# Recurrent chunks of a 64-step linear recurrence: state product and state update moved from level 2 to level 4, GpSimd's operands moved between its mask products

## What is computed

```python
def rwkv7_step(state, inp):
    r_t, w_t, k_t, v_t, kk_t, a_t = inp
    sa = jnp.einsum('bhvk,bhk->bhv', state, -kk_t)
    state = (state * w_t[:, :, None, :] + sa[..., None] * (kk_t * a_t)[:, :, None, :]
             + v_t[..., None] * k_t[:, :, None, :])
    y = jnp.einsum('bhvk,bhk->bhv', state, r_t)
    return state, y
```

## Time and profile before

| | us |
|---|---|
| median of 3 runs | 2630.66 (2630.11 to 2630.99) |
| the profiled execution | 2630.19 |
| its span in the profile | 2628.2 |
| TensorE, matmul busy | 2567.8 (98%) |
| TensorE, weight loads busy | 2086.1 (79%) |
| VectorE busy | 1561.6 (59%) |
| ScalarE busy | 1108.6 (42%) |
| GpSimd busy | 425.6 (16%) |
| recurrent chunks, from the first to the last (2256 to 2509 us) | 253: weight loads busy 207.27 |

### The profile page before, as it was taken

How to read it: one execution, slowest core, us unless ns; L and a number is a source line. 1 busy time by engine, 2 the same in 40 slices (tenths; PEclk the granted TensorE clock), 3 DMA queues, 4 the chain that set the end, 5 groups by cost and what they waited for, 6 DMA issues and landing times.

```text
span 2628.2 us, 46698 instructions
## 1 busy us (share of the span) xinstructions
PE 2567.8 (98%) x19224; PEld 2086.1 (79%) x19224; DVE 1561.6 (59%) x2521; ACT 1108.6 (42%) x2067; POOL 425.6 (16%) x381
## 2 busy tenths in 40 slices
PE   8999999999999999999999999999999999999998
PEld 6887777778778998899888777766776677788876
DVE  8765443436686665676546676355567646656754
ACT  3242233323355543556335554324445545344521
POOL 4421221100000000000000000111112100456644
PEclk9999999999999999999999999999999999999999
DMA  6753443134423454534534222631011253100032
GB/s 227 212 119 107 97 131 101 65 115 165 160 102 116 144 192 141 189 132 150 170 127 173 76 96 90 270 129 49 29 49 49 85 189 105 42 19 19 19 129 96
DMA packets 80754, 307.24 MB, mean 117 GB/s; under 512 B 7200, under 2 KB 8864, under 8 KB 62624
## 3 DMA queue, kind: packets, MB, share of 16 engines
q1 hardware_dynamic: 55984, 238.72, 25.9%
q0 software_dynamic: 12800, 33.56, 5.6%
q10 hardware_dynamic: 11760, 31.99, 3.2%
HBM read 268.32 MB, written 69.47 MB: 129 GB/s over the span
## 4 chain that ended last, share of the span: by engine, by line
PE 83%; DVE 9%; ACT 4%; issue 3%; DMA 1%; POOL 1%; DVEq 0%; ACTq 0%; SPq 0%; POOLq 0%
PE ps L425 46%; PE ps L3270 4%; PE ps L1258 4%; PE ps L1257 4%; PE ps L1259 4%; PE ps L2145 2%; PE ps L2191 2%; PE ps L2171 2%; PE ps L2072 2%; PE ps L609 2%; PE ps L635 1%; PE ps L2074 1%; PE ps L2073 1%; PE ps L624 1%; DVE parts L404 1%
## 5 line engine op out<-in xcount | busy, mean ns | idle before, releaser
L425 PE MATMUL ps<-parts,parts 128*128 128x512 f32 (+2 forms) x6456 | 1467.5, 387 | 15.9 <-DVE parts L804 8.8
L425 PEld LDWEIGHTS ps<-parts,parts 128*128 128x128 f32 x6456 | 1171.6, 188 | 299.7 <-issue 34.3
L404 DVE TENSOR_TENSOR parts<-ring,parts 128x1024 fp32r<-128x1024 f32 x180 | 220.8, 1238 | 174.7 <-ACT parts L381 166.3
L381 ACT CAST parts<-ring 128x1024 fp32r<-128x1024 f32 x183 | 188.7, 1044 | 116.9 <-DMA ring<-in_weights 62.1
L1257 PE MATMUL ps<-parts,parts 128*128 128x256 f32 x840 | 236.2, 281 | 1.3 <-ACT phase_data L1406 1.3
L1258 PE MATMUL ps<-parts,parts 128*128 128x256 f32 x840 | 236.1, 281 | 0.0
L1259 PE MATMUL ps<-parts,parts 128*128 128x256 f32 x840 | 236.0, 281 | 0.0
L404 POOL TENSOR_TENSOR parts<-ring,parts 128x1024 fp32r<-128x1024 f32 x62 | 153.2, 2472 | 423.1 <-DVE parts L381 423.0
L2552 POOL TENSOR_TENSOR phase_data<-phase_data,stream 128x512 f32<-128x512 f32 x12 | 17.2, 1436 | 1186.2 <-PE ps L2082 1186.2
L867 DVE TENSOR_TENSOR_SCAN stream<-stream 128x513 f32<-128x513 f32 (+3 forms) x96 | 95.2, 992 | 173.2 <-ACT stream L737 173.0
L1257 PEld LDWEIGHTS ps<-parts,parts 128*128 128x128 f32 x840 | 158.7, 189 | 2.4 <-ACT phase_data L1406 1.5
(11 more groups left out here) (391 smaller groups left out, 3761.6 us busy)
## 6 DMA issues: line engine op xcount, KB each, us to landing
ring<-in_weights SPq DMA_DIRECT2D x128, 1024.0 KB, 4.9
up_sums<-in_weights POOLq DMA_DIRECT2D x24, 1024.0 KB, 8.9
ring<-in_weights SPq DMA_DIRECT2D x32, 512.0 KB, 4.3
ring<-up_sums SPq DMA_DIRECT2D x30, 512.0 KB, 5.9
phase_data<-up_sums SPq DMA_DIRECT2D x60, 256.0 KB, 5.6
up_sums<-up_sums POOLq DMA_DIRECT2D x8, 1024.0 KB, 5.4
phase_data<-in_weights SPq DMA_DIRECT2D x30, 256.0 KB, 5.5
raw_keep<-phase_scratch SPq DMA_DIRECT2D x21, 256.0 KB, 2.4
```

Of the source, the lines that this page charges most:

```text
L381: cast(self.hi(p), self.whole(p)).then_inc(self.k.hi_ready, 1)
L404: g.tensor_tensor(self.lo(p), self.whole(p), self.hi(p).bitcast(F32), ALU.subtract).then_inc(self.k.lo_ready, 1)
L425: last = pe.matmul(out, a, b, start=i == 0 and a is ah and b is bh, stop=i == len(pairs) - 1 and a is al)
```

## The change

`state_product(c - 1)` on TensorE and `next_state(c - 1)` on VectorE go from level 2 to level 4. `mean` goes from behind level 3 to behind level 4, with its wait as it was. On GpSimd the operands of the next chunk are made after the masks of levels 0 to 2 and before those of 3 to 5, and `bonus_in` and `lower` stand behind the masks. The wait for `x_mm` stays ahead of the first mask. No product is added or left out.

```diff
@@ -3378,11 +3378,12 @@
                     inv_x(c, l)
                     if l == 2 and c >= 1:
                         y_part(c - 1)
-                        state_product(c - 1)
                     if l == 3 and c + 1 < C:
                         raw(c + 1)
+                    if l == 4 and c >= 1:
+                        state_product(c - 1)
                     inv_w(c, l)
-                    if l == 3 and 8 <= c < 12:
+                    if l == 4 and 8 <= c < 12:
                         mean(c - 8)
                     if l == 3 and 9 <= c < 13:
                         bonus(c - 9)
@@ -3619,7 +3620,7 @@
-                    if l == 2 and c >= 1:
+                    if l == 4 and c >= 1:
                         next_state(c - 1)
@@ -3684,15 +3685,16 @@
         for c in range(C):
+            if c >= 2:
+                g.wait_ge(x_mm[1], LEVELS * (c - 1))
+            chunk_levels(k, g, chunk, c, range(0 if c else 1, 3))
+            if c + 1 < C:
+                operands(c + 1)
+            chunk_levels(k, g, chunk, c, range(3, LEVELS))
             if 8 <= c < 12:
                 bonus_in(c - 8)
             if c >= 12:
                 pieces.lower(g, c - 11)
-            if c >= 2:
-                g.wait_ge(x_mm[1], LEVELS * (c - 1))
-            chunk_levels(k, g, chunk, c, range(0 if c else 1, LEVELS))
-            if c + 1 < C:
-                operands(c + 1)
```

## The result

| | before | after |
|---|---|---|
| median of the runs, us | 2630.66 (2629.71 to 2631.09, 5 runs) | 2641.10 (2639.62 to 2643.78, 5 runs) |
| the profiled execution, us | 2630.19 | 2643.78 |
| its span, us | 2628.2 | 2641.9 |

The change makes the kernel slower: the ratio is 1.0041, with a 95% interval of 1.0027 to 1.0056, or +10.4 us. The forecast was 2635.4 (+4.7), in a range of 2631.5 to 2642.5. The time is in the range, and slower was the side with the larger chance, by 0.49 to 0.48.

The account below looks back on a forecast made before the run. The chunks were taken as a loop over TensorE, VectorE and ScalarE. Terms 0.4 + 5.77 - 0.56 - 1.0 + 0.1 = +4.7 us on 2630.19, plus 0.47 to the median, gave 2635.4 us, range 2631.5 to 2642.5.

Parts of the forecast that it names:

- The filler and the loop: Chunks 1 to 7 and 14: state product between x_4 and w_4, less 0.46 us saved in level 2; +0.05 us each.
- Mean's wait: Chunks 8 to 11, level 4: TensorE stands before mean until VectorE's update of the same chunk; together +5.77 us.
- the sum of chunk 9: Chunk 9, level 4 to the next chunk's state_part: 8.66 us instead of 7.22, +1.44; chunks 10 and 11 taken alike.
- The rival: Chunks 1 to 8 and 14: update's multiply waits for GpSimd's second mask, +0.66 us each, +5.9 together, 2641.3; chance 0.22.
- the missed turn: VectorE's update multiply, if 0.10 us later than thought, is let in only after GpSimd's second mask; +0.66 us per chunk.
- Chunks 12 and 13: No mean; VectorE comes late to the next chunk's start; about +0.1 us together, half a microsecond either way.
- Chunk 14: Counted with chunks 1 to 7 as a chunk without mean, +0.05 us.
- Chunks 0 and 15: Chunk 0: first raw's wait for GpSimd's operands goes, -0.56 us. Chunk 15: x_4's wait for the update's multiply shrinks, -1.0.
- the 1.48: Chunk 15: x_4's wait in us for the update's multiply before the change; it should be gone.
- the forecast's own case: Whole kernel: the summed terms hold, 2635.4 us with a spread of about 1.5 us; chance 0.68.

Follow-up runs that it names:

- the filler kernel: Changed kernel plus unread 128 x 512 products right ahead of mean, one in chunk 8, two in each of 9 to 11: 2639.84 us, ratio 1.0036.
- the kernel of the three repairs: Changed kernel with mean in PSUM bank 1, GpSimd's masks of chunks 10 to 13 behind the update, and x_keep's reload later: 2631.16 us, ratio 1.0002.
- The masks kernel: The filler kernel with GpSimd's masks of chunks 10 to 13 waiting for the update of chunks 9 to 12: 2637.58 us, ratio 1.0028.

## Why the prediction was right or wrong

**The filler and the loop** (+0.05 in each of the eight chunks without mean): right. x_4 to w_4 came out at 1.40, and chunks 1 to 7 grew by 0.06. Costing the product at 0.62 plus 0.07 for the change of tile, less what the copy hides, was the right reading.

**Mean's wait** (+5.77 in chunks 8 to 11): right in mechanism, and in size where nothing was on top of it, in chunk 8 (+1.45 forecast, +1.50 measured). Two kernels, one with mean in another bank and one with the old order there, are each only 2.5 to 2.8 us over before, and mean without the wait gives 16.04 and 17.73 in chunks 8 and 9, before's periods. What the forecast left out is that the wait makes TensorE idle long enough to be answered by the clock, and that VectorE's update, on which the wait hangs, has to share the SBUF with GpSimd.

**The step that failed** is the sum of chunk 9, "then 2.57 + 1.91 + 1.28", and "Chunks 10 and 11 as 9" behind it. Its 2.57 is the multiply at 0.42 and was 3.08; its 1.91 holds at full clock only. It forecast +1.44; without half clock it is +1.95 (19.73 against 17.78, in the filler kernel and, with no filler, in chunk 9 of the two kernels with `lower` at the end and with the reload later). The rival's mechanism, the missed turn, is this 0.5. I put the rival's question in chunks 1 to 8 and 14, where the multiply was in time: the next mask's record starts 0.037 us after it in chunk 2 and only 0.005 us after it in chunk 8. It was decided in chunks 9 to 12, which the rival didn't count. There the masks start at w_3 + 4.00, but inv_w of level 4 comes later: between w_3 and w_4 stands bonus, and w_3 to w_4 is 3.36 us (2408.18 - 2404.82) instead of 2.53. The multiply asks at w_3 + 5.41 and meets the third mask, not the first. The rival had the rule right for two tensor_tensor and looked at one place only. The masks held back until the update brought mean to w_4 + 2.54 from 3.08, and with mean in bank 1 holding back the masks is worth 0.94 in chunk 10 (18.67 against 17.73) and 0.56 in chunk 11 (18.67 against 18.11), for the multiply and finish's last step together.

**Left out: the clock.** Two stretches at 0.51 cost 1.6 us each in the profiled execution, 3.2 together, and one in the kernel with GpSimd's old loop. That they follow from the idle time before mean is shown by the filler, which fills it with useless work and shortens chunks 9 and 10, and by the kernels without the wait: at least one stretch in chunks 9 or 10 in each of the four kernels with the wait of 2.06 us, none in chunks 8 to 12 of the five without it. Each of these is one profiled execution. How often an execution has one or two of them is open; so is how much of the median they make, and the filler kernel's median (1.2 us below the kernel beside it) speaks for less than 3.2.

**Chunks 12 and 13** (+0.1, half a microsecond either way): 12 came out at -0.04, 13 at +0.89. 0.5 of it is finish's multiply, held for 2.65 us by `lower`; the place was named for split_lo in chunk 15 and not priced here. GpSimd's new loop is not what does it: with the old loop the multiply is held for 2.89 us and chunk 13 takes 16.73, with the new loop and the update in level 2 it takes 15.86. Counted from chunk 13's turn, `lower` starts at 5.08 before and 4.85 now, the multiply at 4.61 before and 5.11 now, since x_1 waits 0.85 us at the chunk's start. So it has come to stand second. What is left, 0.35 to 0.4, is not isolated: state_part waits 0.30 us for the update at the chunk's end, and in the kernel of the three repairs, where x_1 waits 0.18, `lower` holds finish's second step for 2.01 us instead.

**Chunk 14** (in the forecast with +0.05): +1.15. The forecast followed SP's reload of mix_keep and never looked at the one of x_keep, whose start waits for finish. It came 1.2 us later against the chunk, and the next instruction load arrived only at its end. The run with the reload in chunk 15 shows that the stop belongs to the reload. That TensorE waits for code that queued behind the reload's packets is inferred from the 2.3 to 2.5 us between load and restart in seven kernels; the trace doesn't say whose code a q8 packet is. The masks kernel, with the same place of the reload and no stop, shows that it depends on where the loads fall.

**Chunks 0 and 15.** Chunk 0: -0.56 forecast, -0.60 measured. Chunk 15: the 1.48 is gone, but x_1 waits 0.86 us instead of 0.18 at its start, and state_part 0.28 for the update; from the turn to the first load by w_out (L425) it is 14.43 instead of 14.96, -0.5 for the forecast's -1.0. With level 4 in chunk 15 alone it is 13.70, -1.26: x_1's wait is 0.18 there, so the waits at the start come from level 4 in chunk 14. That update and split_lo stand together in it is the likely reason.

By the terms, against +12.0 in the chunks and behind them: mean 5.8, missed turn 1.5, clock 3.2, chunks 13 and 14 2.0, chunks 1 to 7 0.5, chunk 0 -0.6, chunk 15 and behind -0.3, together 12.1. That the total came near the rival's 2641.3 is chance: of some 7 us beyond the forecast in this execution, 1.5 is the rival's kind of wait in other chunks and the rest clock, `lower`, code and chunk 15. It is luck, too, that the range held: the forecast's own case was to spread by 1.5 us, the median is 5.7 above it, and the upper bound was set for a wait that didn't occur where the rival had it.

## What to carry to other kernels

Before a step with a semaphore is moved, list who waits for its end, down to the DMA issues: here a mean, the next chunk's state_part and a 1 MB reload all hung on the update, and the reload was not priced. A wait on TensorE has a price of its own size and then perhaps a second one, when the clock answers the idle time. Where two engines take turns at SBUF, a margin of some tens of nanoseconds in one chunk (37 ns in chunk 2, 5 in chunk 8, missed by 44 in chunk 9) says nothing of the next: compute it in each kind of chunk, and look for a way to put the one that is waited for first.

## What the runs showed of the hardware that I had not expected

- A VectorE tensor_scalar, one SBUF tensor and a per-partition operand in SBUF, is held by GpSimd's tensor_tensor just as the tensor_tensor is: 128 x 64 takes 0.25 us at the least and 0.76 beside masks of 0.73. Four small ones wait four times. The Trainium skill (SBUF — State Buffer, Who interferes with whom) counts tensor_scalar among the operations that can take both port pairs. The trace agrees. An add with one operand in PSUM (L3591, 0.41 to 0.42) was not held in the same place.
- The two engines take turns, and the one that comes later bears the wait in its own duration: the multiply 0.96 us in chunk 9, the second mask 0.97 in chunk 2. Over all kernels with the one multiply, none of the 34 was let ahead where the next mask's record began 0.041 us or more before it, and all 87 were where it began 0.001 us before it or later. That the second mask had ended 5 ns earlier, as in chunk 9, was no opening.
- Beside GpSimd's tensor_scalar the hold is not the whole instruction, as the prediction takes it for every GpSimd instruction that reads SBUF, and the multiply's 0.42 in the kernel before wasn't always owed to an idle GpSimd. In its chunks 7 and 8 the multiply started 0.8 us into such an instruction (L3673, 1.56 us) and took 0.42; in chunk 15 of the changed kernel it started 0.12 us into one (L3674, 1.56 us) and took 0.84, ending 0.6 us before it.
- TensorE's granted clock fell to 0.51 (1.2 GHz) for 3.4 us beside waits of 2.06 us in chunks 9 or 10, in all four kernels that have these waits: twice in the changed kernel, once in the others. The kernel with four tensor_scalar, whose waits before mean are 3.1 to 3.5 us, has six such stretches in its chunks, one of them 6.8 us long. It did not fall in chunk 8, with a wait of 1.6, nor in chunk 11, with 2.06 again.
- TensorE stopped for 1.0 to 1.6 us in the middle of a loop behind a 1 MB reload on another queue, in seven kernels, and went on 2.3 to 2.5 us after the start of a 16 KB packet on the instruction queue q8. Its stop moved from chunk 14 to 15 with the reload.
